# Kernel study: the diagonal 32x32 blocks of the GDN inverse solved on GpSimd beside the local attention

## The chip, the core and the metric

The kernel runs on one core of a Trainium2 chip. The metric is device time in microseconds (us), the median of several runs; here 2867.46 us over three runs (2866.38 to 2867.61). The profile is one execution with its own span.

## The reference, cut to what matters

Two transformer blocks in float32 on 512 positions. The change is in the even layer of the second, which has a gated delta rule (GDN, 6 heads of width 128) beside a dilated local attention. The delta rule solves, for each head and chunk of positions, a unit lower triangular system:

```
decay = jnp.exp(jnp.where(incl, gam[..., :, None] - gam[..., None, :], -jnp.inf))
kk = jnp.einsum('bhnid,bhnjd->bhnij', kc, kc)
lower = jnp.eye(c) + jnp.where(strict, bc[..., :, None] * kk * decay, 0.0)
sol = lax.linalg.triangular_solve(lower, rhs, left_side=True, lower=True, unit_diagonal=True)
...
delta = u_n - jnp.einsum('bhck,bhkv->bhcv', w_n, state)
o_n = jnp.einsum('bhck,bhkv->bhcv', qd_n, state) + jnp.einsum('bhij,bhjv->bhiv', qk_n, delta)
state = gl_n[..., None, None] * state + jnp.einsum('bhck,bhcv->bhkv', kd_n, delta)
```

## The kernel before

The program is a row of regions, each with a barrier of all five engines behind it: a region ends when its last engine ends, and SyncE has to have issued its DMAs. Inside a region each engine has its own list of instructions, in order, with semaphores between them. Three regions and the start of a fourth matter here.

**The residual region** ends with the projections of the even layer. Weights come in pieces of 128x1024: SyncE loads them into one of three `raw` buffers (`W.load`, L205), ScalarE rounds them to a high part (`split_high`, L220), VectorE or GpSimd forms the rest (`split_low`, L230), into four buffers each. A load into a used `raw` waits for the low part three pieces earlier. At this region's end the first four pieces of the next projection (`even_out`) are already split and three more are loaded.

**The window region** (`window_region`) is the local attention: 8 units, each with scores (L1476, L1480) on TensorE, logits on VectorE, exponentials on ScalarE, 12 transposes (`turn`, L1491) and 24 products with the values (L1509). SyncE brings bias tables, level masks and the small table `pick`. GpSimd has no work here.

**The recurrence region** (`recurrence_region`) walks four chunks (n = 0 to 3) of 128 positions, with the six heads in two groups g of three. For a chunk it needs the inverse of the 128x128 triangular matrix I - M. `MT` holds M transposed, `TT` the transposed inverse, `T` the inverse. Level 0 sets 2x2 blocks (`first_level`, L2613 and L2616); each of the levels 1 to 6 doubles the size of the finished diagonal blocks:

- GpSimd masks `MT` into `BT` (`masked`, L2721);
- TensorE multiplies `T` with `BT` (`a`, L2366), ScalarE copies the result to `W1` (`product`, L2497);
- TensorE multiplies `W1` with `TT` (`b`, L2374), VectorE adds that to `TT` (`sums`, L2642);
- TensorE transposes `TT` (`turn_inverse`, L2380) and ScalarE copies it to `T` (`inverse`, L2502); not on level 6.

In the spaces of the levels (`beside`) TensorE runs the state steps of the chunk before (s1 to s4 and `head_sums`, L2317 to L2356) and the preparation of the chunk after (p1 to p7, L2248 to L2303), all in PSUM banks 6 and 7. The preparation needs copies by ScalarE (`decays`, `betas`, `key_rows` L2470, `value_rows` L2481, `inverse_start` L2490), sums by VectorE (`decays`, `kept`, `matrix`, `scores`, `queries`, `keys`) and products by GpSimd (`factors` L2731, `decayed_betas` L2737). Chunk 0 is prepared ahead of the loop, the prologue. Behind chunk 3 there is a tail: one long logarithm on ScalarE (L2564), then `delta`, `output`, `square` and the last logarithms (L2572).

**The layer region** starts with `even_out`, whose first products (L292) need split weights.

A three-head product of two 128x128 matrices shows as six matmul records in the trace, since each float32 matmul is two; a three-head transpose shows as three. In the order listings below, which count instructions as written, both are x3.

## Time and profile before

| | us |
|---|---|
| median of three runs | 2867.46 |
| profiled execution, first to last instruction | 2866.3 |
| TensorE busy | 2653.8 (93%) |
| VectorE busy | 1494.4 (52%) |
| ScalarE busy | 1085.4 (38%) |
| GpSimd busy | 438.2 (15%) |
| window region | 62.0 (1485.1 to 1547.1) |
| recurrence region | 174.8 (1547.1 to 1721.9) |

Times inside the span are counted from its first instruction. The two regions are 8% of the span. Busy shares of the whole program say little about them: what counts there is how full TensorE is in each stretch, and which engine a region's last instruction waits for.

### The profile page before, as it was taken

To read this page: it belongs to the slowest core of one execution; us is meant where nothing else is said; L and a number is where in the kernel's file an instruction comes from. 1 tells how busy PE (TensorE), PEld (TensorE's weight loads), DVE (VectorE), ACT (ScalarE), POOL (GpSimd) and SP (SyncE) were. 2 spreads that over 40 slices of the span, in tenths; PEclk is the share of its full clock that TensorE was granted. 3 is DMA by queue.
4 is the path that set the end of the run, shared out by engine and by line. 5 is a ranking of instruction groups with operands and counts; after the bars stand their busy time and mean duration, and the time that the engine had idled before them with its cause. 6 is when DMAs were issued, how large, how long until landed. Compare 5 with 4: busy or idle time off the path is not lost. (4 is left out here: it accounts for less than half of the span.)

```text
span 2866.3 us, 32688 instructions
## 1 busy us (share of the span) xinstructions
PE 2653.8 (93%) x12838; PEld 2117.6 (74%) x12838; DVE 1494.4 (52%) x2141; ACT 1085.4 (38%) x1659; POOL 438.2 (15%) x356
## 2 busy tenths in 40 slices
PE   8998998799999999969988998999998988899997
PEld 5676887577778888746777886887776865687775
DVE  5644553454456653365434545677634345676743
ACT  5653443533432322334323454322224446422223
POOL 4544442000000000000001433000020031200002
PEclk9998899999999999989998999999999999999999
DMA  6233002333023323222220001222332310122231
GB/s 216 92 107 118 1 1 84 112 103 103 23 88 103 96 90 94 74 74 74 81 88 1 1 1 52 81 88 91 108 95 93 96 45 30 57 90 89 88 109 61
DMA packets 82624, 222.06 MB, mean 77 GB/s; under 512 B 13293, under 2 KB 29949, under 8 KB 81283
## 3 DMA queue, kind: packets, MB, share of 16 engines
q1 hardware_dynamic: 78112, 205.49, 22.4%
q10 hardware_dynamic: 4360, 14.49, 1.4%
q8 instruction: 103, 1.69, 0.2%
q14 instruction: 49, 0.40, 0.0%
HBM read 213.60 MB, written 11.58 MB: 79 GB/s over the span
## 5 line engine op out<-in xcount | busy, mean ns | idle before, releaser
L230 DVE TENSOR_TENSOR w_low<-w_raw,w_high 128x1024 fp32r<-128x1024 f32 (+2 forms) x341 | 410.8, 1206 | 874.2 <-ACT w_high L220 874.0
L292 PE MATMUL bank<-x_high,w_high 128*128 128x512 f32 x1840 | 742.7, 404 | 32.2 <-DVE x_low L486 20.4
L293 PE MATMUL bank<-x_low,w_high 128*128 128x512 f32 x1840 | 734.5, 399 | 0.0
L294 PE MATMUL bank<-x_high,w_low 128*128 128x512 f32 x1840 | 731.2, 397 | 0.0
L220 ACT ACTIVATE w_high<-w_raw 128x1024 fp32r<-128x1024 f32 (+2 forms) x380 | 386.3, 1019 | 620.5 <-PE bank L294 502.4
L292 PEld LDWEIGHTS bank<-x_high,w_high 128*128 128x128 f32 x1840 | 349.0, 190 | 142.4 <-issue 53.0
L293 PEld LDWEIGHTS bank<-x_low,w_high 128*128 128x128 f32 x1840 | 349.0, 190 | 87.8 <-issue 5.5
L294 PEld LDWEIGHTS bank<-x_high,w_low 128*128 128x128 f32 x1840 | 348.6, 189 | 83.1
L294 PE MATMUL bank<-f_high,w_low 128*128 128x512 f32 x528 | 209.9, 397 | 0.0
L292 PE MATMUL bank<-f_high,w_high 128*128 128x512 f32 x528 | 208.8, 395 | 0.9 <-DVE w_low L230 0.9
L293 PE MATMUL bank<-f_low,w_high 128*128 128x512 f32 x528 | 208.4, 395 | 0.0
L292 PEld LDWEIGHTS bank<-f_high,w_high 128*128 128x128 f32 x528 | 99.1, 188 | 27.1 <-issue 3.0
L293 PEld LDWEIGHTS bank<-f_low,w_high 128*128 128x128 f32 x528 | 99.1, 188 | 25.3 <-issue 0.5
L294 PEld LDWEIGHTS bank<-f_high,w_low 128*128 128x128 f32 x528 | 99.1, 188 | 23.2
L230 POOL TENSOR_TENSOR w_low<-w_raw,w_high 128x1024 fp32r<-128x1024 f32 x39 | 95.3, 2443 | 127.4 <-ACT w_high L220 127.3
L403 POOL TENSOR_TENSOR ln_half<-x 128x512 f32<-128x512 f32 x4 | 6.9, 1718 | 690.9 <-DVE x L3672 690.9
L3585 ACT ACTIVATE f_high<-gate 128x512 fp32r<-128x512 f32 x44 | 27.8, 632 | 215.0 <-DVE gate L3703 215.0
L292 PE MATMUL bank<-o_high,w_high 128*128 128x512 f32 x192 | 79.4, 414 | 10.3 <-DVE o_low L555 10.3
L3582 ACT ACTIVATE gate<-gate 128x512 f32<-128x512 f32 x44 | 27.8, 632 | 155.1 <-DVE gate L717 155.1
L293 PE MATMUL bank<-o_low,w_high 128*128 128x512 f32 x192 | 78.1, 407 | 0.0
L294 PE MATMUL bank<-o_high,w_low 128*128 128x512 f32 x192 | 77.9, 406 | 0.0
L1022 DVE TENSOR_TENSOR raw<-bank,rstd 128x512 f32<-128x512 f32 x38 | 25.9, 687 | 95.2 <-PE bank L294 75.8
(605 smaller groups left out, 4090.2 us busy)
## 6 DMA issues: line engine op xcount, KB each, us to landing
w_raw<-in_ffn_in_dram SPq DMA_DIRECT2D x132, 512.0 KB, 3.3
w_raw<-in_ffn_out_dram SPq DMA_DIRECT2D x48, 512.0 KB, 3.5
w_raw<-in_gdn_in_dram SPq DMA_DIRECT2D x24, 512.0 KB, 3.3
w_raw<-in_mix_in_dram SPq DMA_DIRECT2D x22, 512.0 KB, 4.3
w_raw<-in_ffn_out_dram SPq DMA_DIRECT2D x24, 384.0 KB, 3.1
w_raw<-in_swa_qk_dram SPq DMA_DIRECT2D x12, 512.0 KB, 3.3
bias_rows<-bias_row ACTq DMA_DIRECT2D x4, 1280.0 KB, 13.8
w_raw<-in_mix_gate_a_dram SPq DMA_DIRECT2D x8, 512.0 KB, 3.3
```

The costliest lines, as they stand in the source:

```text
L220: self.nc.scalar.activation(self.high[c % SPLIT][:, 0:w], self.raw[c % RAW][:, 0:w], ACT.Copy).then_inc(self.high_done, 1)
L230: (on or self.nc.vector).tensor_tensor(self.low[c % SPLIT][:, 0:w], self.raw[c % RAW][:, 0:w], self.high[c % SPLIT][:, 0:w].bitcast(F32), ...
L292: nc.tensor.matmul(out, wh, high[:, k, :], start=first + at == 0, stop=False)
L293: nc.tensor.matmul(out, wh, low[:, k, :], start=False, stop=False)
L294: last = nc.tensor.matmul(out, wl, high[:, k, :], start=False, stop=first + at == depth - 1)
L403: self.nc.gpsimd.tensor_tensor(self.half[:], self.x[:, 0, :], self.x[:, 1, :], ALU.add).then_inc(self.S["half_ok"], 1)
L1022: W.freed(nc.vector.tensor_tensor(raw[i % 3][:], W.bank(PS, name, n)[:], rstd[:], ALU.mult), name, n)
L3582: nc.scalar.activation(g[i % 2][:], g[i % 2][:], ACT.Silu).then_inc(R["act_ready"], 1)
L3585: nc.scalar.activation(FH[:, i, :], g[i % 2][:], ACT.Copy).then_inc(R["f_high"], 1)
```

## The change

1. **Window region.** TensorE also computes K K^T for the four 32x32 diagonal blocks of every head and chunk (`key_edges`: 96 matmuls of 32x32 outputs) between the first and the second scores. ScalarE copies them out. SyncE writes `gam` and `beta` to HBM and reads them back by block (2 and 8 DMAs), writes the blocks to HBM in runs of 128 bytes (4 DMAs) and reads them back as 96 partitions of 1024 numbers, one block in each. GpSimd forms decays and signs, and solves the 96 unit triangular blocks by forward substitution (`solve_edges`: 30 steps of a product and a sum). The result goes to HBM and comes back as `TC` (1 and 4 DMAs, the last four waited for in the next region). The scratch for it is the memory of the high and low weights.
2. **Residual and recurrence region, weights.** The four pieces of `even_out` are therefore split in the recurrence region: ScalarE in slots 3 to 6 of the last chunk, GpSimd at its own end.
3. **Recurrence region.** Two doubling levels are left (32 to 64, 64 to 128). Each chunk has seven slots; slot s holds p(s+1) of the chunk after, and the state steps of the chunk before stand in slots 0 to 3 and 5. The p steps use banks 1 and 4. `first_level` is one product that spreads the solved blocks. GpSimd makes both masks of a group together, in the order factors, masked, decayed_betas.

The diff below is cut to its core; each `@` names the function and the engine, and long arguments are shortened.

```diff
@solve_edges
+    for j in range(1, EDGE - 1):
+        w = EDGE - 1 - j
+        part = TMP[rows, 0:j * w].rearrange("p (s t) -> p s t", t=w)
+        pool.wait_ge(step, j)
+        nc.gpsimd.tensor_tensor(part, X[:, 0:j, j:j + 1].broadcast_to(both), X[:, j:j + 1, j + 1:].broadcast_to(both),
+                                ALU.mult).then_inc(product, 1)
+        pool.wait_ge(product, j)
+        nc.gpsimd.tensor_tensor(X[:, 0:j, j + 1:], X[:, 0:j, j + 1:], part, ALU.add).then_inc(step, 1)
@window_region, sync
+            sp.wait_ge(R["keys_copied"], 2)
+            for b in range(B):
+                sp.dma_start(inner["keys_flat"][b].rearrange("m s t -> s m t"), ...).then_inc(R["keys_out"], 16)
+            sp.wait_ge(R["keys_out"], 16 * B)
+            sp.dma_start(KB[rows, :], inner["keys_flat"].rearrange("b m s t -> (b m) (s t)")).then_inc(R["keys_in"], 16)
+            sp.wait_ge(R["solved"], 1)
+            sp.dma_start(inner["solved_flat"].rearrange("b m s t -> (b m) (s t)"), SOL[rows, :]).then_inc(...)
+            sp.wait_ge(R["solved_out"], 16)
+            for b in range(B):
+                sp.dma_start(TC[...], inner["solved_flat"][b].rearrange("m s t -> s m t")).then_inc(inner["solved_in"], 16)
@window_region, scalar
+                if u == 1:
+                    act.wait_ge(R["gap"], 2)
+                    nc.scalar.activation(DEC[rows, :], DEC[rows, :], ACT.Exp).then_inc(R["edge_decay"], 1)
@recurrence_region, tensor
+                for slot in range(7):
+                    for g in range(G):
+                        if slot == 0: a(n, 0, g)
+                        if slot == 1: b(n, 0, g)
+                        if slot == 2: turn_inverse(n, g)
+                        if slot == 3: a(n, 1, g)
+                        if slot == 4: b(n, 1, g)
+                        if before >= 0: ...   # s1, s2, s3, s4, -, head_sums in slots 0 to 5
+                        if after < NT:
+                            (p1, p2, p3, p4, p5, p6, p7)[slot](after, g)
@recurrence_region, scalar
+                    if after == NT and slot >= 3:
+                        W.split_high(act, W.end("swa_v") + slot - 2)
@recurrence_region, vector
-                nc.vector.tensor_tensor(TT, MT, mask[:, 0:1, :], ALU.mult)
-                nc.vector.tensor_tensor(TT, TT, C["ident"], ALU.add)
+                nc.vector.tensor_tensor(TT, edges[:, a:b, n, None, :].broadcast_to(shape), mask[:, 0:1, :], ALU.mult)
@recurrence_region, gpsimd
+                for g in range(G):
+                    factors(n, g)
+                for g in range(G):
+                    masked(n, g)
+                    decayed_betas(n, g)
+            pool.wait_ge(R["tt0"], at(NT - 1, G - 1))
+            W.split_low(pool, W.end("swa_v") + SPLIT, nc.gpsimd)
@residual_region
-            W.load(sp, W.end("swa_v") + SPLIT + RAW)
+            W.load(sp, W.end("swa_v") + RAW)
-                W.split_high(act, W.ahead("swa_v", gr))
+                W.split_high(act, min(W.ahead("swa_v", gr), W.end("swa_v")))
```

TensorE at the start of the window region before (scores of units 0 and 1, the turn of unit 0):

```order
L1476 MATMUL bank<-swa_qk_6800 128x512 x2
L1480 MATMUL bank<-swa_qk_6800 128x128 x4
L1476 MATMUL bank<-swa_qk_6800 128x512 x2
L1480 MATMUL bank<-swa_qk_6800 128x128 x4
L1491 MATMUL bank<-ident,window_logits_12173 128x128 x12
```

and after, where the 96 products of `key_edges` (L1578) stand between the scores of the first two units:

```order
L1529 MATMUL bank<-swa_qk_6808 128x512 x2
L1533 MATMUL bank<-swa_qk_6808 128x128 x4
L1578 MATMUL bank<-qkvz_6810 32x32 x96
L1529 MATMUL bank<-swa_qk_6808 128x512 x2
L1533 MATMUL bank<-swa_qk_6808 128x128 x4
L1546 MATMUL bank<-ident,window_logits_12160 128x128 x12
```

The turn of unit 0 (L1491 before, L1546 after) is now behind 96 more matmuls.

TensorE in chunk 1 before, level 1 and the start of level 2 (L2366 is `a`, L2374 is `b`, L2380 `turn_inverse`, L2317 s1, L2248 p1 and L2250, L2251 its small parts, L2326 s2):

```order
L2366 MATMUL bank<-t_12756,bt_12757 128x128 x3
L2317 MATMUL bank<-state_12765,qkvz_6802 128x128 x3
L2366 MATMUL bank<-t_12756,bt_12757 128x128 x3
L2317 MATMUL bank<-state_12765,qkvz_6802 128x128 x3
L2374 MATMUL bank<-tt_12752,w_243_12758 128x128 x3
L2248 MATMUL bank<-gam_6804,pick_12172 128x128 x3
L2250 MATMUL bank<-ident,gam_6804 128x6
L2251 MATMUL bank<-ident,beta_6803 128x6
L2374 MATMUL bank<-tt_12752,w_243_12758 128x128 x3
L2380 MATMUL bank<-ident,tt_12752 128x128 x3
L2248 MATMUL bank<-gam_6804,pick_12172 128x128 x3
L2380 MATMUL bank<-ident,tt_12752 128x128 x3
```

and after, slots 0 and 1 (L2449 is `a`, L2457 `b`, L2403 s1, L2349 p1, L2410 s2, L2359 p2):

```order
L2449 MATMUL bank<-t_13017,bt_13018 128x128 x3
L2403 MATMUL bank<-state_13026,qkvz_6810 128x128 x3
L2349 MATMUL bank<-gam_6812,pick_12152 128x128 x3
L2351 MATMUL bank<-ident,gam_6812 128x6
L2352 MATMUL bank<-ident,beta_6811 128x6
L2449 MATMUL bank<-t_13017,bt_13018 128x128 x3
L2403 MATMUL bank<-state_13026,qkvz_6810 128x128 x3
L2349 MATMUL bank<-gam_6812,pick_12152 128x128 x3
L2457 MATMUL bank<-tt_13014,w_251_13019 128x128 x3
L2410 MATMUL bank<-rhs_13023,tt_13013 128x128 x3
L2359 MATMUL bank<-beta_6811,pick_12152 128x128 x3
L2457 MATMUL bank<-tt_13014,w_251_13019 128x128 x3
```

`a` and `b` are now in different slots, with three more steps of both groups between them, and no transpose stands in the first two slots.

ScalarE at the end of chunk 3 before (L2497 `product`, L2524 `sums_read`, L2564 the long logarithm, L2509 `delta`):

```order
L2497 ACTIVATE w_243_12758<-bank 128x384
L2524 ACTIVATE qkvz_6802<-bank 128x3x128
L2497 ACTIVATE w_243_12758<-bank 128x384
L2524 ACTIVATE qkvz_6802<-bank 128x3x128
L2502 ACTIVATE t_12756<-bank 128x384 x2
L2497 ACTIVATE w_243_12758<-bank 128x384 x2
L2564 ACT_TABLE_LOAD
L2564 ACTIVATE qkvz_6802<-qkvz_6802,rms_eps 128x6x384
L2509 ACTIVATE delta_12763<-bank 128x384 x2
```

and after (L2564 is now `product`, L225 the high part of a weight piece, L2592 `sums_read`, L2635 the long logarithm, L2577 `delta`):

```order
L2564 ACTIVATE w_251_13019<-bank 128x384
L2588 ACTIVATE rhs_13023<-o_even_12150 128x384
L225 ACTIVATE w_high_5_49<-w_raw_1 128x1024
L225 ACTIVATE w_high_6_50<-w_raw_2 128x1024
L2592 ACTIVATE qkvz_6810<-bank 128x3x128 x2
L225 ACTIVATE w_high_7_51<-w_raw_3 128x1024
L225 ACTIVATE w_high_8_52<-w_raw_1 128x1024
L2635 ACT_TABLE_LOAD
L2635 ACTIVATE qkvz_6810<-qkvz_6810,rms_eps 128x6x384
L2577 ACTIVATE delta_13024<-bank 128x384 x2
```

Four pieces of weights now stand ahead of the long logarithm, and the fourth uses `w_raw_1` a second time.

## Rows read from the trace of the kernel before

**Rows 1.** Stretches: window region, prologue, chunks 0, 1 and 3.

```profile
core 0: us, PE busy (x) PEld busy (x) DVE busy (x) ACT busy (x) POOL busy (x), PEclk, DMA share, GB/s
1485.06:1547.10 62.04, 54.99 (x392) 48.48 (x392) 25.40 (x88) 26.96 (x51) 0.01 (x1) 0.91 0.08 21
1547.10:1567.50 20.40, 17.12 (x70) 14.53 (x70) 10.79 (x23) 6.91 (x23) 7.39 (x7) 0.50 0.00 0
1567.50:1603.20 35.70, 32.15 (x246) 29.28 (x244) 18.50 (x34) 16.79 (x46) 16.85 (x16) 0.96 0.00 1
1603.20:1639.90 36.70, 35.26 (x288) 32.84 (x287) 20.64 (x43) 18.19 (x46) 14.41 (x14) 1.00 0.01 2
...
1676.60:1713.80 37.20, 35.98 (x290) 32.72 (x288) 17.50 (x31) 21.45 (x50) 15.07 (x14) 1.00 0.00 1
```

**Rows 2.** The longest wait in total in the four chunks, 1567 to 1714.

```profile
POOL bt L2721 <- PE bank L2366: 73.0, 35, 4.7
```

**Rows 3.** TensorE weight loads in order of time (start, us, what), chunk 1.

```profile
1612.25 0.75 PEld L2366 LDWEIGHTS bank<-t,bt 128*128 128x128 f32 x6
1612.92 0.75 PEld L2326 LDWEIGHTS bank<-rhs,tt 128*128 128x128 f32 x6
...
1624.23 0.36 PEld L2380 LDWEIGHTS bank<-ident,tt 128*128 128x128 f32 x3
1624.57 0.75 PEld L2344 LDWEIGHTS bank<-delta,k_rows 128*128 128x128 f32 x6
```

**Rows 4.** ScalarE in order of time, end of the residual region.

```profile
1480.49 1.06 ACT L220 ACTIVATE w_high<-w_raw 128x1024 fp32r<-128x1024 f32 x1 [4.58 <-PE bank L317]
```

**Rows 5.** TensorE on 32-column products in order of time, and that stretch's clock.

```profile
2327.53 1.93 PE L2916 MATMUL bank<-k_about,q_blocks 128*32 128x128 f32 x32
...
2327.00:2330.00 3.00, 2.47 (x36) 1.38 (x32) 0.47 (x1) 0.63 (x4) 1.45 (x4) 0.50 0.02 5
```

**Rows 6.** TensorE in order of time, first turn of the window.

```profile
1492.42 2.74 PE L1491 MATMUL bank<-ident,window_logits 128*128 128x128 f32 x12
```

**Rows 7.** DMA: issues by SyncE, packets from 20 to 30 us, landing of 512 KB.

```profile
1485.06 3.65 SPq L1464 DMA_DIRECT2D g_bias<-bias_rows  x8
...
q1 hardware_dynamic: 3026, 1.23, 45.7%
...
w_raw<-in_gdn_in_dram SPq DMA_DIRECT2D x24, 512.0 KB, 3.3
```

**Rows 8.** GpSimd groups by shape: busy, mean ns, idle before.

```profile
L230 POOL TENSOR_TENSOR w_low<-w_raw,w_high 128x1024 fp32r<-128x1024 f32 x39 | 95.3, 2443 | 127.4 <-ACT w_high L220 127.3
...
L2845 POOL TENSOR_TENSOR k_about<-k_far,far_decay 128x224 f32<-128x224 f32 x4 | 2.6, 656 | 0.0
...
L2845 POOL TENSOR_TENSOR k_about<-k_far,far_decay 128x64 f32<-128x64 f32 x4 | 1.2, 296 | 0.0
```

**Rows 9.** GpSimd in order of time, 2367 to 2370.

```profile
2367.25 0.72 POOL L2832 TENSOR_TENSOR k_about<-k_near,gla_qkr 128x256 f32<-128x256 f32 x1
2368.12 1.53 POOL L2838 TENSOR_TENSOR q_blocks<-q_about,gla_qkr 64x256 f32<-64x256 f32 x2
```

**Rows 10.** One instruction each of ScalarE, GpSimd, VectorE in chunk 1.

```profile
1621.19 0.49 ACT L2497 ACTIVATE w<-bank 128x384 f32<-128x384 f32 x1 [0.18 <-PE bank L2366]
...
1621.24 1.00 POOL L2721 TENSOR_TENSOR bt<-mt,level_mask 128x384 f32<-128x384 f32 x1 [1.57 <-PE bank L2366]
...
1623.21 0.56 DVE L2642 TENSOR_TENSOR tt<-tt,bank 128x384 f32<-128x384 f32 x1 [2.40 <-PE bank L2374]
```

**Rows 11.** ScalarE in order of time: value rows of chunk 1, end of chunk 3, tail.

```profile
1601.80 0.97 ACT L2481 ACTIVATE v_rows<-bank,col 128x128 f32<-128x128 f32 x3
...
1712.25 1.28 ACT L2564 ACT_TABLE_LOAD   x1
...
1715.67 0.85 ACT L2509 ACTIVATE delta<-bank 128x384 f32<-128x384 f32 x2
...
1721.29 0.58 ACT L2572 ACTIVATE qkvz<-bank,rms_eps 128x384 f32<-128x384 f32 x1 [0.59 <-PE bank L2356]
```

More of the change, by code:

```diff
@@ L1458, in window_region @@
     with region(nc, "bias0", "bias1", "scores", "near", "logits", "exp", "turned", "copied", "copied_last", "inv", "values", "rows", "final",
-                "o") as (block, R):
+                "o", "keys", "keys_copied", "flat", "edge_gates", "keys_out", "keys_in", "covered", "gap", "edge_decay", "signed",
+                "product", "step", "solved", "solved_out") as (block, R):
         @block.sync
@@ L1516, in finish, with key_edges @@
                 last.then_inc(R["final"], 1)
+            def key_edges():
+                for m in range(M):
+                    h, n = m // NT, m % NT
+                    for b in range(B):
+                        k = K[:, h, n * P + EDGE * b:n * P + EDGE * b + EDGE]
+                        last = nc.tensor.matmul(
+                            PS[4 + m // 16][EDGE * b:EDGE * b + EDGE, EDGE * (m % 16):EDGE * (m % 16) + EDGE], k, k,
+                            start=True, stop=True)
+                    if m in (15, M - 1):
+                        last.then_inc(R["keys"], 1)
             for u in range(N + 2):
@@ L2666, in gated @@
                                                of(3, n, g), ALU.mult, ALU.mult).then_inc(R["og"], 1)
-            for prepare in (decays, kept, matrix, first_level, scores, queries, keys):
+            for prepare in (decays, kept, matrix, scores, queries, keys, first_level):
                 for g in range(G):
@@ L2672, in _ @@
                 before, after = n - 1, n + 1
[L2673 to L2689 removed]
+                for slot in range(7):
@@ L2703, in _ @@
-                        if before >= 0 and level == 5 and after < NT:
+                            if slot == 5:
+                                keys(after, g)
+                        if slot == 4:
+                            sums(n, 1, g)
+                        if after < NT and slot == 4:
+                            queries(after, g)
+                            first_level(after, g)
+                        if before >= 0 and slot == 5:
                             gated(before, g)
+                        if after == NT and slot == 6:
+                            rhs(n, g)
```

443 lines of the change are left out of this document (228 added, 215 removed).

## Prediction

> **What bounds the kernel now.** I read the table by stretches first. In chunks 1 and 3 of the recurrence TensorE is busy 35.3 of 36.7 us and 36.0 of 37.2 us at full clock [rows 1]; in the other engines' columns of the same rows nothing exceeds 22 us. So the loop is bound by TensorE's own list of work, and the waits say the same from the other side: GpSimd's masks wait for TensorE, 73 us in total [rows 2]. The pitch of that list is in the weight loads: a three-head product starts 0.67 us after the one before it, a three-head transpose is followed after 0.34 us [rows 3]. Whatever work is taken from TensorE there comes off the time, until a chain of waits is longer. The window region is different: 62.0 us, GpSimd empty, VectorE and ScalarE under half [rows 1]. It is free for GpSimd, but its barrier waits for SyncE and GpSimd too, and the change gives both a long chain.
>
> **The change, part by part.** The sum is made in the profiled execution (2866.3 us); the median of the runs is 1.2 us above it.
>
> *Residual region.* The high part of a weight piece at 1480.49 stands ahead of the last copies [rows 4]; it goes, and they start when TensorE ends at 1480.4. -1.0 us, below 0 and not under -2: nothing is added there.
>
> *Window region.* I count T from its start (before: next region at T = 62.0). TensorE's new 96 products are 192 records. The nearest row is a 32-column product, 32 records in 1.93 us at half clock, (1.93 - 0.27) / 31 = 0.054 us each [rows 5]. That gives 10.3 us (bounds 5 at full clock, 21 if the column groups don't overlap: 0.11 us each), from T = 3.0 to 13.3, copied at 14.1. The first turn then starts near T = 15.5, not 7.4 [rows 6]: the attention ends 8.1 us later, less some 1.5 us for a turn and scores that ran at half clock before and may be at full clock by then, and the next region could start at T = 68.7.
>
> The chain of the blocks: four DMAs of 768 runs, issued at 3.65 / 8 = 0.46 us each from T = 14.2. Small packets took 0.457 x 160 us / 3026 = 24 ns of one engine [rows 7], so 3072 take 4.6 us over 16 engines; with 2.0 us to land, T = 20.8 (bounds 0 and +7 for packets up to 60 ns). The read back lands 3.3 us after its issue [rows 7]: T = 24.5. Decays and signs (8 DMAs behind `flat`, three passes over 1024 numbers, one exponential) I put ready at T = 23, so not last. First product, 128x1024: 2.44 us [rows 8], T = 27.0. Then 60 instructions over 9920 numbers in all. From 64 to 224 numbers costs (656 - 296) / 160 = 2.25 ns each, fixed part 0.15 us [rows 8]: 60 x 0.15 + 9920 x 0.00225 = 31.3 us. Each waits for the one before it; the gap in such a place is 2368.12 - 2367.97 = 0.15 us, and 0.07 inside the pair behind it [rows 9]: 0.1 x 60 = 6.0. T = 64.3. Diagonal, write back (3.3), four issues (1.8), barrier (0.9): T = 70.8. The chain is last, by 2 us over the attention. Window region +8.8 us, bounds +4 (solve at 28, key products at full clock) and +23 (gaps 0.15, slow packets, 0.1 us more per instruction).
>
> The Trainium skill ("DMA: Bandwidth & Descriptors", Specifications) says that transfers under 512 bytes are done as read-modify-write. The small packets of [rows 7] are loads into SBUF; no row here shows small stores to HBM, of which the change makes 3072. If stores took twice as long, the sum would be 4.6 us higher. It speaks against the change but does not turn it; it is a rival below.
>
> *Recurrence, prologue.* 20.4 us before [rows 1]. GpSimd now makes four masks ahead of the second `decayed_betas` (2 x 1.0 us more), `keys` and then `first_level` follow it. I follow the chain: second mask pair done 2.3 us later than the old `decayed_betas`, first_level cheaper. +2.4 us (0 to +5). The landing of `TC` (issued before the barrier, some 7 us) is hidden by the 20 us of this prologue; if it weren't, it would cost what it is late.
>
> *Chunks.* Removed per chunk: 4 levels x 2 groups x (a and b) = 16 products x 0.67 = 10.7 us, 8 transposes x 0.34 = 2.7 us. TensorE's list for a full chunk is 36.7 - 13.4 = 23.3 us including the stalls of before, about 22.0 by counting: 26 products, 8 transposes, 2 head sums and small parts. Then I walked the seven slots with each engine's durations (ScalarE 0.49, GpSimd 1.0, VectorE 0.56 [rows 10], and up to 1.0 for what reads two SBUF tiles). Slots 0 to 4 run without a stall: `b` of a group comes 3 us after its `a`, and the copy between takes 0.7. In slots 5 and 6 TensorE has only 2.6 us of work, while ScalarE must do key rows, sums and value rows of both groups, 0.97 us for each set of rows [rows 11]: transpose, rows, transpose, `t`. There the second group's last transpose waits for `v_rows`. +1.6 us: 23.8 us per full chunk, for chunks 1 and 2: 2 x -12.9 = -25.8 us (each between 22.2, TensorE's list alone, and 30, where every slot takes the 4.3 us of the fullest).
>
> Chunk 0 has no state steps, so its TensorE list is only 14 us and the chain of preparation steps sets the time: 18.4 us by the same walk. It starts at half clock as before (0.50 in the prologue, [rows 1]), for which I add 3.6: 22.0 for 35.7, -13.7 us (18.5 to 29).
>
> Chunk 3 and tail were 1676.6 to 1721.9 = 45.3 us. Now: five slots of `a`, `b`, state steps end near 13 us, but ScalarE has four weight pieces ahead of the long logarithm. The fourth uses a `raw` that SyncE may fill only when GpSimd has done the first low part: high at 13.2, low 2.44 us [rows 8] at 15.7, load 3.3 us [rows 7] at 19.0, high 1.06 [rows 4] at 20.1. Then the table load and the logarithm, 1715.67 - 1712.25 = 3.4 us, and `delta` starts at 23.6; from there to the end 1721.9 - 1715.7 = 6.2 us as before [rows 11]. 29.8 us: -15.5 (bounds -19, if the load is early enough, and -12). Half of what the removed levels could give is lost here to a new wait for a load.
>
> Sum: -1.0 + 8.8 + 2.4 - 13.7 - 25.8 - 15.5 = -44.8; 2866.3 - 44.8 = 2821.5, and 1.2 more for the median: 2822.7 us, 1.6% faster. I say 2823. Its own range is 2812 to 2835.
>
> **Rivals.**
> - *The attention hides the chain and the chunks run at TensorE's list.* Window +4, chunks 1 and 2 at 22.2, chunk 3 -19, chunk 0 -17: about 2808. For it: the chain is last by 2 us only. Against it: the two-engine chains in slots 5 and 6.
> - *GpSimd is dearer on narrow rows than on rows of 16 numbers.* L2845 has inner rows of 16; the solve goes down to 1. With 0.3 us more on each of 60 instructions the chain ends at T = 89, net -27: 2841.
> - *Small stores are slow*: +4.6 us by the price above, 2827.
> - *The recurrence becomes bound by latency, or TensorE falls to half clock in it.* The clock was 0.50 in all of the prologue, where TensorE stalled [rows 1]. Full chunks of 30 us, chunk 0 of 29, chunk 3 two more, near the upper bound of each part: +21, 2844. Against it: the walk finds one stall of 1.6 us.
> - *Slower than before.* The place is the barrier of the window region: each microsecond by which GpSimd's solve is longer goes straight to the end. The gain elsewhere is 53.6 us, so the region would have to end at T = 115.6, the solve at 82 us, 1.37 us for each instruction. The nearest rows are 0.30 and 0.66 us [rows 8]. At 1.5 us each: solve 90 us, 2876. Only a new kind of cost could do it.
>
> **Chances.** Forecast 0.55; attention hides it 0.12; narrow rows 0.11; small stores 0.06; latency or clock 0.12; slower 0.03; something else, near no change, 0.01. The range 2807 to 2845 leaves out the last two and the ends of the others. 0.2% (6 us) is about what a measurement can tell from no change. Faster 0.96, same 0.01, slower 0.03.
>
> **What would show it.** The next region starts 70 to 72 us after the window region's start, GpSimd's last add is the last wait there, and its adds and products take 0.2 to 0.7 us. The 192 small records take about 10 us and the first turn starts near T = 15.5. Full chunks take 23 to 25 us with TensorE above 90% until `key_rows`. ScalarE waits for `w_raw` ahead of the fourth high part. The forecast is wrong if GpSimd's gaps or durations are twice these, if TensorE's clock is 0.5 in a chunk, or if VectorE waits for `TC` at the end of the prologue.

## The result, and the profile after

The changed kernel takes 2821.23 us (median of 4 runs, 2820.41 to 2827.58), the kernel before 2867.49 in the same session: ratio 0.9837, 95% interval 0.9821 to 0.9852, 1.6% faster. The profiled execution is 2820.41 us with a span of 2818.6. Forecast were 2823 and 2807 to 2845.

The table of stretches of the changed kernel: window region, prologue, chunks 0, 1 and 2, and all from chunk 3 to the start of the next region. They answer to [rows 1]; columns as there.

```profile
1481.78:1547.80 66.02, 59.08 (x584) 51.81 (x584) 25.30 (x88) 28.66 (x54) 42.02 (x72) 0.89 0.18 41
1547.80:1569.77 21.97, 16.70 (x70) 14.34 (x70) 9.04 (x21) 6.91 (x23) 9.30 (x9) 0.58 0.00 1
1569.77:1595.23 25.46, 24.18 (x125) 21.68 (x125) 10.97 (x24) 10.02 (x30) 7.35 (x7) 0.65 0.00 1
1595.23:1619.64 24.41, 23.62 (x191) 21.58 (x189) 15.20 (x34) 13.51 (x38) 9.42 (x10) 1.00 0.00 1
1619.64:1644.14 24.50, 23.71 (x190) 21.67 (x189) 16.40 (x36) 13.50 (x38) 8.99 (x9) 1.00 0.01 1
...
1644.14:1676.14 32.00, 23.36 (x173) 20.82 (x171) 15.34 (x24) 19.70 (x32) 11.13 (x5) 0.95 0.20 66
```

The last stretch ends here with the first product of the next region, in the kernel before at 1724.60:

```profile
1676.60:1724.60 48.00, 42.14 (x329) 37.46 (x328) 20.18 (x35) 28.84 (x61) 15.07 (x14) 0.99 0.00 1
```

The forecast took it to the last logarithm (1721.9) on both sides, which leaves the change comparable.

Against the kernel before (us):

| stretch | before | after | change | forecast |
|---|---|---|---|---|
| up to the window region | 1485.06 | 1481.78 | -3.3 | -1.0 |
| window region | 62.0 | 66.0 | +4.0 | +8.8 |
| prologue | 20.4 | 22.0 | +1.6 | +2.4 |
| chunk 0 | 35.7 | 25.5 | -10.2 | -13.7 |
| chunks 1 and 2 | 73.4 | 48.9 | -24.5 | -25.8 |
| chunk 3 to the next region | 48.0 | 32.0 | -16.0 | -15.5 |
| the rest | 1141.7 | 1142.5 | +0.8 | 0 |

The first row is no clean result: eleven experiments run the same program up to there, and their window regions start between 1483.09 and 1490.74. Nor is the size of the second: in seven profiles that leave this region alone, the changed kernel's among them, it takes 63.8 to 66.2 us, and in a second profile of the old region 61.0. The full chunks are what was forecast: TensorE 23.6 of 24.4 us busy at full clock. The places that deserve a look are the window region, whose +4.0 hides two errors, and chunk 0, where the granted clock is 0.65. That clock is no accident of one execution: the eight profiled kernels with the changed kernel's orders in prologue and chunk 0 take 25.1 to 25.8 us for chunk 0.

GpSimd in the window region of the changed kernel, in order of time: the decays, the first product, the first step and the last sum. Only GpSimd's rows are shown; a bracket holds the idle time ahead of a row and what ended it.

```profile
1495.86 2.77 POOL L1697 TENSOR_SCALAR edge_decay<-edge_decay 96x1024 f32<-96x1024 f32 x1
1499.87 2.37 POOL L1700 TENSOR_TENSOR edge_decay<-edge_decay,edge_gates 96x1024 f32<-96x1024 f32 x1 [1.24 <-ACT edge_decay L1625]
1502.38 2.35 POOL L1704 TENSOR_TENSOR edge_inverse<-edge_blocks,edge_decay 96x1024 f32<-96x1024 f32 x1
1504.81 0.23 POOL L1456 TENSOR_TENSOR edge_part<-edge_inverse 96x30 f32<-96x30 f32 x1
1505.12 0.23 POOL L1459 TENSOR_TENSOR edge_inverse<-edge_inverse,edge_part 96x30 f32<-96x30 f32 x1
...
1539.09 0.26 POOL L1459 TENSOR_TENSOR edge_inverse<-edge_inverse,edge_part 96x30 f32<-96x30 f32 x1
...
1547.80 0.74 POOL L2781 MEMSET state<- 128x768 f32 x1 [8.23 <-POOLq L551]
```

The substitution takes 34.5 us, from 1504.81 to 1539.35, not 37.3: the gap between two dependent instructions is 0.08 us, the cheapest takes 0.23. The last product and sum, 30 rows of one number, take 0.25 and 0.26 us, the first, one row of 30, 0.23 each: narrow rows cost next to nothing. But GpSimd then waits 8.23 us at the barrier. SyncE, behind it, is done at T = 62.8 (T from the region's start); the region ends at T = 66.0. So the solve isn't last in this execution. TensorE and ScalarE in the same region show what is:

```profile
1484.75 1.93 PE L1578 MATMUL bank<-qkvz 128*32 128x32 f32 x192
...
1489.36 1.53 PE L1546 MATMUL bank<-ident,window_logits 128*128 128x128 f32 x12 [0.16 <-ACT edge_keys L1621]
...
1500.79 4.22 PE L1564 MATMUL bank<-swa_v,window_turned 128*128 128x64 f32 x24 [0.95 <-issue]
1504.80 2.77 PE L1546 MATMUL bank<-ident,window_logits 128*128 128x128 f32 x12
...
1545.05 0.66 PE L1570 MATMUL bank<-ident,window_rows 128*128 128x128 f32 x4 [0.45 <-DVE window_rows L1660]
```

```profile
1498.66 1.06 ACT L1625 ACTIVATE edge_decay<-edge_decay 96x1024 f32<-96x1024 f32 x1 [5.70 <-POOL edge_decay L1697]
1499.63 1.06 ACT L1601 ACTIVATE window_turned<-bank 128x512 f32<-128x512 f32 x2
...
1545.74 1.07 ACT L1629 ACTIVATE o_even<-bank 128x512 f32<-128x512 f32 x1 [4.63 <-PE bank L1570]
```

The 192 key records take 1.93 us, 0.010 us each, at a granted clock of 0.94; in the kernel with the products done twice, below, they ran at 0.50 and took 2.79 us. The first turn starts at T = 7.6 (before: 7.4). What holds the attention is ScalarE's 5.70 us of waiting for GpSimd's decays, in front of the copies of unit 1 (1499.63). TensorE, which turned that unit at 1496.25 to 1497.73, stands idle behind them and then does the next transposes in 2.77 us instead of 1.48, at half clock.

The prologue and the start of chunk 0, TensorE in order of time, and the granted clock (seventh value, ahead of the DMA share) in pieces of 4 us:

```profile
1564.02 0.55 PE L2385 MATMUL bank<-ident,qkvz 128*128 128x128 f32 x3 [0.21 <-ACT k_rows L2537]
1568.32 1.51 PE L2392 MATMUL bank<-ident,tt 128*128 128x128 f32 x6 [3.76 <-DVE tt L2687]
1569.77 1.65 PE L2449 MATMUL bank<-t,bt 128*128 128x128 f32 x6
```

```profile
1560.00:1564.00 4.00, 3.73 (x16) 2.69 (x15) 2.08 (x5) 1.81 (x7) 2.07 (x3) 0.57 0.00 0
1564.00:1568.00 4.00, 0.55 (x3) 0.31 (x3) 2.10 (x3) 1.51 (x6) 3.05 (x3) 0.86 0.00 0
1568.00:1572.00 4.00, 3.68 (x15) 3.14 (x16) 0.64 (x2) 1.47 (x3) 0.00 (x0) 0.50 0.00 0
...
1584.00:1588.00 4.00, 4.00 (x23) 4.00 (x23) 1.58 (x3) 1.52 (x5) 2.00 (x3) 0.58 0.00 0
```

TensorE waits 3.76 us for the solved blocks in TT, which VectorE copies only behind the keys, and these wait for GpSimd's second decayed betas. The clock rises to full shortly ahead of this wait, falls back within it (near 1567), and stays at half until 1587: 17 of the 25.5 us of chunk 0, in which TensorE is busy all the time.

The tail, ScalarE from the fourth high part on, and VectorE's products ahead of rhs:

```profile
1662.71 1.06 ACT L225 ACTIVATE w_high<-w_raw 128x1024 fp32r<-128x1024 f32 x1 [2.83 <-DMA w_raw<-in_even_out_dram]
1663.79 1.28 ACT L2635 ACT_TABLE_LOAD   x1
1665.08 2.22 ACT L2635 ACTIVATE qkvz<-qkvz,rms_eps 128x2304 f32<-128x2304 f32 x1
1667.20 0.85 ACT L2577 ACTIVATE delta<-bank 128x384 f32<-128x384 f32 x2
```

```profile
1657.63 4.90 DVE L2739 SCALAR_TENSOR_TENSOR o_even<-o_even,gdn_norm,qkvz 128x384 f32<-128x384 f32 x2
1662.45 1.00 DVE L2725 TENSOR_TENSOR rhs<-v_rows,bank 128x384 f32<-128x384 f32 x2
...
1670.45 0.62 DVE L2739 SCALAR_TENSOR_TENSOR o_even<-o_even,gdn_norm,qkvz 128x384 f32<-128x384 f32 x1 [6.99 <-ACT rhs L2588]
```

The wait for the fourth weight piece is there, and `delta` starts 23.1 us into chunk 3 (23.6 forecast). The first row of VectorE is two products in 4.90 us; the same product takes 0.62 at 1670. GpSimd's four low parts (1657.13 to 1667.05) run beside the slow ones. `rhs`, which has one of its two inputs in PSUM, runs beside them too and takes 0.50 us each.

### The profile page after: what moved, and what is told of

Read it like the earlier page. It is cut to its first block and busy times, and to the rows that moved or that the text cites. A ratio compares the mean times of both kernels' runs of the same rounds, so it can differ in the third digit from the quotient of the medians.

```text
span 2818.6 us, 31986 instructions
## 1 busy us (share of the span) xinstructions
PE 2605.4 (92%) x12550; PEld 2070.7 (73%) x12550; DVE 1464.8 (52%) x2097; ACT 1057.6 (38%) x1598; POOL 457.9 (16%) x399
## 5 line engine op out<-in xcount | busy, mean ns | idle before, releaser
L297 PE MATMUL bank<-x_high,w_high 128*128 128x512 f32 x1840 | 746.9, 406 | 32.1 <-DVE x_low L491 20.4
L225 ACT ACTIVATE w_high<-w_raw 128x1024 fp32r<-128x1024 f32 (+2 forms) x380 | 386.2, 1019 | 603.1 <-PE bank L299 502.0
L235 POOL TENSOR_TENSOR w_low<-w_raw,w_high 128x1024 fp32r<-128x1024 f32 x43 | 105.2, 2448 | 141.1 <-ACT w_high L225 141.0
L297 PE MATMUL bank<-o_high,w_high 128*128 128x512 f32 x192 | 78.4, 408 | 10.3 <-DVE o_low L560 10.3
L1027 DVE TENSOR_TENSOR raw<-bank,rstd 128x512 f32<-128x512 f32 x38 | 25.8, 686 | 96.6 <-PE bank L299 77.2
```

What stands on the lines that cost most here:

```text
L225: self.nc.scalar.activation(self.high[c % SPLIT][:, 0:w], self.raw[c % RAW][:, 0:w], ACT.Copy).then_inc(self.high_done, 1)
L235: (on or self.nc.vector).tensor_tensor(self.low[c % SPLIT][:, 0:w], self.raw[c % RAW][:, 0:w], self.high[c % SPLIT][:, 0:w].bitcast(F32), ...
L297: nc.tensor.matmul(out, wh, high[:, k, :], start=first + at == 0, stop=False)
L1027: W.freed(nc.vector.tensor_tensor(raw[i % 3][:], W.bank(PS, name, n)[:], rstd[:], ALU.mult), name, n)
```

## The experiments

Times are set against the 2821.23 us of the changed kernel; sizes of a few us are read from the stretches of the profiles, since runs of one kernel spread by up to 7 us.

### Is the solve last in the window region?

**Solve shortened** (28 of its 30 steps left out):

```diff
-    for j in range(1, EDGE - 1):
+    for j in (1, 2):
```

> The changed kernel with 2 of the 30 steps of the substitution (4 of 60 GpSimd instructions); the other steps are left out, so the blocks are not inverses. GpSimd's chain ends 30 us earlier. Theory A (the attention, held by the wait for the decays, ends last): the region stays at 66.0 us (within 0.5), and the total near 2821. Theory S (the solve's chain ends last): the region shrinks by what the chain stood over the attention, 2 us by the prediction, more if the attention had not been delayed.

Measured: the region keeps 66.16 us, while GpSimd now waits 41.48 us at the barrier. 2823.09 us. Its attention was last, and theory S, my prediction's own, is out for it: the last transposes start at T = 63.4, as in the changed kernel. Two executions further down with the changed kernel's own orders in this region had the solve last.

```profile
1484.29:1550.45 66.16, 59.06 (x584) 52.03 (x585) 25.31 (x88) 28.66 (x54) 13.19 (x16) 0.89 0.18 41
```

**Every product twice:**

```diff
+        for i in range(2):
-        nc.gpsimd.tensor_tensor(part, X[:, 0:j, j:j + 1].broadcast_to(both), X[:, j:j + 1, j + 1:].broadcast_to(both),
-                                ALU.mult).then_inc(product, 1)
-        pool.wait_ge(product, j)
+            nc.gpsimd.tensor_tensor(part, X[:, 0:j, j:j + 1].broadcast_to(both), X[:, j:j + 1, j + 1:].broadcast_to(both),
+                                    ALU.mult).then_inc(product, 1)
+            pool.wait_ge(product, 2 * j - 1 + i)
```

> The changed kernel with every product of the substitution done twice, each waiting for the one before it: 90 GpSimd instructions for 60. The second product gives the same numbers. The 60 took 34.5 us with gaps of 0.08 us, so the 30 more should add about 17 us to the solve. Theory A: the chain of the solve (last issue at T = 62.8) stood 2 to 3 us ahead of the attention's end, so the region grows by 17 - 3 = about 14 to 15 us, to 80 to 81, and GpSimd or SyncE is the last wait. If the solve's chain was already last (theory S), the region grows by the whole 17 us. If wider gaps or a wait of another kind bound each instruction, the added time per product differs from 0.57 us.

Measured: 2840.86 us. SyncE's issue behind the solve comes at T = 74.7 (1563.65 - 1488.93) instead of 57.8: 16.9 us for 30 products, 0.56 each with its gap. The region grows by 14.7 us, so 2.2 us of the solve had been hidden in the changed kernel's profile; beyond that each microsecond goes to the end, as the rival "slower" had it. ScalarE waits for the decays here too, 5.18 us, but TensorE stays at full clock behind the wait, and its last transposes start at T = 58.6 (1547.50 - 1488.93) instead of 63.3.

```profile
1547.50 0.66 PE L1571 MATMUL bank<-ident,window_rows 128*128 128x128 f32 x4 [0.45 <-DVE window_rows L1661]
...
1488.93:1569.69 80.76, 55.24 (x585) 48.62 (x585) 25.31 (x88) 28.43 (x54) 56.51 (x102) 0.84 0.14 33
```

**The exponential of the decays behind the copies of unit 1** (ScalarE):

```diff
                 if 1 <= u <= N:
                     copies(u - 1)
+                if u == 2:
+                    act.wait_ge(R["gap"], 2)
+                    nc.scalar.activation(DEC[rows, :], DEC[rows, :], ACT.Exp).then_inc(R["edge_decay"], 1)
                 if u < N:
                     exponentials(u)
...
-                if u == 1:
-                    act.wait_ge(R["gap"], 2)
-                    nc.scalar.activation(DEC[rows, :], DEC[rows, :], ACT.Exp).then_inc(R["edge_decay"], 1)
```

> The changed kernel with ScalarE's exponential of the block decays moved from behind the exponentials of unit 1 to behind the copies of unit 1 in the window region. ScalarE waited 5.70 us for GpSimd there, and the turned tiles of unit 1, ready at about 1497.3, were copied at 1499.63. Theory A (the attention ended last): the copies start 2.3 us earlier, the exponential still starts at 1498.7, the solve isn't later, and the region shrinks from 66.0 to 64 us (TensorE's last transposes at T = 61.3 instead of 63.3); the solve's last DMA issue at T = 62.8 becomes the near tie. Theory S (my prediction: the solve's chain ends last): the region stays at 66.0, because the chain's end is the same.

Measured: TensorE's last transposes start at T = 57.2 (1542.31 - 1485.13) instead of 63.3. That is 6.1 us, three times the 2.0 expected, because half clock went with the wait: some 3 us right behind it, and 1.6 more in a later stretch (1523 to 1530 in the changed kernel) that the kernel before also had at half clock (1526.20). The region shrinks by 1.3 us only, to 64.73, because now the solve is last: SyncE's last issue ends at T = 63.7, the next region begins 1.0 later. Median 2820.98 (ratio 0.9837, 0.9822 to 0.9851): by itself not to be told from the changed kernel.

```profile
1542.31 0.66 PE L1570 MATMUL bank<-ident,window_rows 128*128 128x128 f32 x4 [0.46 <-DVE window_rows L1660]
...
1485.13:1549.86 64.73, 54.31 (x584) 48.35 (x585) 25.30 (x88) 28.59 (x54) 41.97 (x72) 0.93 0.18 41
```

The comparison of two profiles makes the order look better than it is. Nine kernels of this study keep the changed kernel's order on ScalarE and its 192 records. Their last transposes start at T = 58.6 to 63.4; the half clock behind the wait is there in all but the one with products twice. The wait by itself costs 1.4 us at most (58.6 against 57.2), the rest is the clock. In the kernels with the blocks ahead of the keys and with the wide products first (both below) they start at 60.1 and 60.2, the solve is last, as GpSimd's short wait at the barrier shows, and the region takes 63.8 us, less than with the decays moved:

```profile
1544.49 0.66 PE L1570 MATMUL bank<-ident,window_rows 128*128 128x128 f32 x4 [0.46 <-DVE window_rows L1660]
...
1548.10 0.74 POOL L2781 MEMSET state<- 128x768 f32 x1 [6.02 <-POOLq L551]
...
1484.35:1548.14 63.79, 55.97 (x584) 49.99 (x585) 25.31 (x88) 28.55 (x54) 41.97 (x72) 0.93 0.18 42
```

So in the seven profiles that leave the region alone attention and solve end within 2.5 us of each other, and the later one changes with the clock behind the wait. With the exponential moved the region takes 64.7 us here and 64.2 in the last kernel below, within the 63.8 to 66.2 of the old order: no run shows a gain for the region.

### What does a key product cost?

**Each key product four times:**

```diff
-                        last = nc.tensor.matmul(
+                        for _ in range(4):
+                            last = nc.tensor.matmul(
```

> The changed kernel with each of TensorE's 96 key products done four times: 768 records for 192, all else as it is. The 192 took 1.93 us at full clock. If the price is 0.010 us for one record, the 576 more take 5.8 us and the first turn moves from T = 7.6 to 13.4. The prediction's price, 0.054, would give 31 us more. Theory A: ScalarE's wait for the decays (5.7 us at unit 1) hides 2.3 us or more of it, so the region grows by 2 to 4 us, not 5.8.

Measured: 2841.22 us; the region is 80.07 us. The records of TensorE:

```profile
1490.76 4.70 PE L1579 MATMUL bank<-qkvz 128*32 128x32 f32 x207
1496.73 2.71 PE L1579 MATMUL bank<-qkvz 128*32 128x32 f32 x128 [1.27 <-issue]
1500.20 2.71 PE L1579 MATMUL bank<-qkvz 128*32 128x32 f32 x128 [0.76 <-issue]
```

They take 22.4 us (1490.76 to 1513.16), not 7.7: my expectation was wrong. In the changed kernel the group of 32 columns changes with every product, that is after two records; here 8 records in a row go to the same group, and the pitch is 2.71 / 128 = 0.021 us instead of 0.010, at full clock. The eight also have the same operands and the same output, and no run separates that from the group. And this long list waits for its issue after each 128 records, 0.8 to 1.3 us. The last transposes start 14.0 us later (T = 77.3, 1565.35 - 1488.06), the records take 20.5 us more: ScalarE no longer waits for the decays, as theory A had it, and the half clock behind that wait is gone too.

### What holds chunk 0?

**The stall filled in part** with transposes that nobody reads:

```diff
+            for i in range(13):
+                nc.tensor.transpose(PS[6][:, chunk(i % 3)], C["ident"][:], C["ident"][:])
             for g in range(G):
                 p7(0, g)
```

> The changed kernel with 13 transposes of the identity into an unused bank on TensorE, between the last value transposes of the prologue and the first transpose of TT, where TensorE stood idle for 3.76 us (1564.57 to 1568.32). Nothing else moves; they take about 13 x 0.275 = 3.6 us at half clock. Theory H (half clock): the stall is what kept TensorE at 1.2 GHz until 1587, and chunk 0 (25.5 us) was bound by TensorE at that clock. With the stall filled the clock rises within about 5 us of chunk 0's start, as in the kernel before, and chunk 0 takes 18 to 21 us: 5 to 7 us less, about 2815. Rival K (chain): the chain of preparation steps sets chunk 0, as I predicted, and the clock adds little: chunk 0 stays within 1 us of 25.5 even if the clock rises. Rival N: the clock doesn't depend on this stall: it stays at 0.5 to about 1587, and nothing changes.

**The copies of the solved blocks ahead of the keys** (VectorE, prologue):

```diff
-            for prepare in (decays, kept, matrix, scores, queries, keys, first_level):
+            for prepare in (decays, kept, matrix, scores, queries, first_level, keys):
```

> The changed kernel with one order changed on VectorE: in the prologue of the recurrence the copies of the solved blocks into TT (first_level) stand ahead of the scaling of the keys, which waits for GpSimd's second decayed betas. Direct effect: first_level can run at 1563.0 to 1564.1 instead of 1567.6, TensorE's transposes of TT start near 1564.8 instead of 1568.3 and chunk 0 starts near 1566.3: 3.4 us earlier. Theory H: with the stall gone the clock rises early as well, so chunk 0 is 5 to 7 us shorter too: 8 to 10 us in all, about 2812. Rival N (the clock doesn't follow from the stall): -3.4 only, or, if the rise at 1587 stays where it is, about -1.7, since half of the work moved forward runs at half clock. Rival K (the chain sets chunk 0): -3.4 and chunk 0 still 25 us.

Measured: 2819.89 us (ratio 0.9830, 0.9815 to 0.9845) and 2814.03 us (0.9816, 0.9798 to 0.9834). Prologue and chunk 0 of the first, then of the second:

```profile
1549.33:1570.92 21.59, 17.72 (x83) 15.24 (x83) 9.04 (x21) 7.02 (x24) 9.27 (x9) 0.64 0.00 1
1570.92:1593.05 22.13, 20.85 (x125) 18.68 (x126) 10.98 (x24) 9.94 (x30) 7.36 (x7) 0.77 0.00 1
```

```profile
1548.14:1566.36 18.22, 16.03 (x70) 13.73 (x71) 9.32 (x20) 6.79 (x23) 8.28 (x8) 0.58 0.02 4
1566.36:1588.38 22.02, 20.74 (x126) 18.56 (x125) 12.21 (x26) 10.00 (x30) 8.96 (x9) 0.77 0.00 1
```

In the first kernel the stall was only shortened: the clock had risen ahead of it, so the 13 transposes took 1.58 us (1565.90), not 3.6, and TensorE still waited 2.34 us:

```profile
1569.82 0.99 PE L2392 MATMUL bank<-ident,tt 128*128 128x128 f32 x6 [2.34 <-DVE tt L2691]
```

Chunk 0 is 3.3 and 3.4 us shorter at a clock of 0.77, and the second kernel gains 3.7 in the prologue. Half of theory H: the clock does set chunk 0, but it didn't stay up. In both it rose ahead of the chunk (near 1565 and 1564) and fell again for about 10 us within it. The median of the first isn't to be told from the changed kernel's; the second's is 7.2 us lower, with intervals that just overlap.

**The kernel before, with a stall:**

```diff
+            for t in (R_, U, W1):
+                nc.vector.tensor_tensor(t[:], MT[0][:], MT[0][:], ALU.mult).then_inc(R["late"], 1)
...
+            pe.wait_ge(R["late"], 3)
             for g in range(G):
                 p7(0, g)
```

> The kernel before, with a stall put into the prologue of its recurrence: VectorE does three more products of 768 numbers into tiles that are free there, and TensorE waits for them ahead of the first transposes of TT (at 1566.06 before). They should end near 1569.8, so chunk 0 starts 3.5 to 4 us later. Theory H (TensorE's stall at this place costs the full clock for the first part of chunk 0): the clock, which before rose at about 1570, rises 15 to 20 us later, and chunk 0 takes 6 to 9 us more than its 35.7, so 10 to 13 us in all. Rival N (something else of the change holds the clock, such as GpSimd's or the DMA queues' work): chunk 0 keeps its 35.7 us and only the 4 us of the stall show.

Measured: 2871.13 us. TensorE waits 3.14 us; prologue 23.56 us (+3.2, of which 0.2 is where the stretch was cut), chunk 0 35.96 (+0.3), clock 0.96 as before [rows 1]. Theory H fails in this kernel: a stall at this place is not enough. Here, as in the kernel before, the clock was 0.50 through the whole prologue and rose once, some 4 us after the stall. In the changed kernel it had risen ahead of the stall and fell in it.

```profile
1546.38:1569.94 23.56, 17.16 (x70) 14.67 (x70) 13.40 (x26) 6.91 (x23) 7.41 (x7) 0.50 0.00 1
...
1569.94:1605.90 35.96, 32.41 (x245) 29.56 (x245) 18.49 (x34) 16.79 (x46) 16.86 (x16) 0.96 0.00 1
```

**Wide products first** (the changed kernel, TensorE's order in slot 0 of chunk 0):

```diff
+            for g in range(G):
+                a(0, 0, g)
...
-                        if slot == 0:
+                        if slot == 0 and n:
                             a(n, 0, g)
```

> The changed kernel with both first products a of chunk 0 (128 rows each) ahead of the two spreads of chunk 1 (products with 6 rows), on TensorE alone; the stall of 3.76 us ahead of the first transposes of TT stays. After that stall TensorE then does 4.7 us of 128-row work at half clock without a break, about what the kernel before with a stall put in did (4.2 us) when its clock rose at 26 us after the region's start; in the changed kernel it rose at 39.5. Theory G (the narrow products of chunk 0's first slots, which the seven slots put between the wide ones, keep the clock low): the clock rises at 25 to 28 us and chunk 0 takes 19 to 21 us instead of 25.5. Rival P (what comes first in the chunk doesn't matter, only where the stall lies): the clock stays at half to about 39, and chunk 0 stays at 25 to 26.

Measured: chunk 0 22.26 us at a clock of 0.76; but a median of 2821.87 us (0.9838, 0.9820 to 0.9856), no gain. The clock rises near 1574.7, 25.6 us after the region's start, as theory G had it; but it falls again near 1578 and stays at half to about 1585, which no theory had. What a chunk gains in one profiled execution doesn't show in the median. Inconclusive.

### What holds the tail?

**The logarithm ahead of the third and fourth high part** (ScalarE); in the second kernel also **rhs ahead of the last gated products** (VectorE); in the third the latter alone:

```diff
-                    if after == NT and slot >= 3:
+                    if after == NT and slot in (3, 4):
                         W.split_high(act, W.end("swa_v") + slot - 2)
...
...
             # behind the long logarithm
+            W.split_high(act, W.end("swa_v") + 3)
             for g in range(G):
                 delta(n, g)
+            W.split_high(act, W.end("swa_v") + 4)
```

```diff
-                        if before >= 0 and slot == 5:
+                        if after < NT and before >= 0 and slot == 5:
                             gated(before, g)
                         if after == NT and slot == 6:
                             rhs(n, g)
+                    if after == NT and slot == 6:
+                        for g in range(G):
+                            gated(before, g)
```

> The changed kernel with ScalarE's order at the end of the recurrence changed: two high parts, head sums, then the long logarithm, the third high part, delta of the last chunk, the fourth high part. ScalarE waited 2.83 us for the load of the fourth piece ahead of the table load, and delta started at 1667.20. Theory W (the wait for w_raw, as predicted, sets the tail): delta can start when TensorE has done s2, at 1665.2 to 1666 instead of 1667.2, so the next region starts 1 to 2 us earlier. It can't be the 3 us of the wait, since s2 itself starts only at 1663.05 behind VectorE's rhs. Rival V (VectorE's gated products ahead of rhs set the tail): no change over 0.5 us.

> As the kernel with the logarithm moved ahead of the third and fourth high part, and VectorE's rhs of the last chunk ahead of the two gated products of chunk 2, which took 4.90 us beside GpSimd's low parts (2.45 us each; 0.62 without them) and held rhs until 1662.45. Both ends of the tail are then free: rhs near 1660.4, s2 of TensorE to 1662.5, the logarithm done at 1662.4, the third high part at 1663.5, delta from there: 3.7 us earlier than 1667.2, and the next region starts 3.5 us earlier, if two waits of equal length (V and W) held the tail together. Each alone gives 0 to 1.5. If another wait is behind both (the last low part of GpSimd, which now comes later, or the barrier), less.

> The changed kernel with VectorE's rhs of the last chunk ahead of the two gated products alone; the logarithm stays behind the fourth high part. TensorE's s2 can start 2.5 us earlier, but delta waits for ScalarE, which waits for the load of the fourth weight piece and then does the logarithm (to 1667.2, 23.0 us after the start of chunk 3). If both waits hold the tail in parallel, delta stays where it is and the last stretch keeps 32.0 us (up to 34.4, as other executions of the same orders had). If VectorE's order alone set it, 2.5 us less.

Measured, from chunk 3 to the next region: 30.19, 28.11 and 34.51 us; medians 2822.19 (0.9836, 0.9820 to 0.9853), 2818.01 (0.9821, 0.9805 to 0.9838), and 2830.04 in a single run, whose window region starts 9.0 us later than the changed kernel's, ahead of any change. No median here is clear of the changed kernel's. The changed orders of other experiments leave this stretch alone, and there it takes 32.0 to 34.4 us. The spread lies behind the start of `delta`: from there to the next region it is 8.9 us where the clock stays full and 9.6 to 11.4 in the other executions, at a granted clock of 0.75 to 0.86. The start of `delta` is the cleaner reading. It is 23.1 us into chunk 3 with rhs alone (1676.44 - 1653.37), as without it, where all kernels with the old orders lie at 23.1 to 23.4; 20.6 with the logarithm alone (1667.16 - 1646.57), where ScalarE waits for TensorE's s2 and this for VectorE's rhs; and 19.2 with both (1665.92 - 1646.75). So ScalarE's queue is the last wait, and VectorE's order the one right behind it.

```profile
1653.37:1687.88 34.51, 24.39 (x173) 22.02 (x171) 14.99 (x24) 19.68 (x32) 11.13 (x5) 0.90 0.17 61
```

```profile
1646.75:1674.86 28.11, 22.01 (x172) 19.59 (x171) 14.20 (x24) 19.57 (x32) 10.56 (x5) 1.00 0.23 75
```

### Together

The four new orders in one kernel: decays later, blocks ahead of keys, logarithm first, rhs first.

> The changed kernel with the four new orders together: the exponential of the block decays behind the copies of unit 1, first_level ahead of the keys in the prologue, the logarithm ahead of the third and fourth high part, and rhs ahead of the last gated products. Each has been run on its own or in a pair: the window region went from 66.0 to 64.7 us, prologue and chunk 0 from 47.4 to 40.2, the tail from 32.0 (up to 34.4 in other executions) to 28.1. If they add up: 1.3 + 7.2 + 3.9 = 12.4 us under the changed kernel, about 2809. If the clock gives one of them back in the next stretch (an execution with a tail 2 us longer had the rest of the program 2.3 us shorter), 2811 to 2813. Over 2815 the parts don't add up.

Measured: 2808.01 us (5 runs, 2806.56 to 2812.53), ratio 0.9794, interval 0.9780 to 0.9808, clear of the changed kernel's. It beats both kernels. The total is the expected one, the parts are not: against the changed kernel the window region gives 1.8 us (64.18), prologue and chunk 0 10.2, the tail 2.3 (29.73), where 1.3, 7.2 and 3.9 were expected. `delta` starts 19.2 us into chunk 3 as before; the tail's rest is the spread named above. End of the prologue and chunk 0:

```profile
1547.27:1561.00 13.73, 12.54 (x54) 11.73 (x55) 4.83 (x15) 3.10 (x10) 4.83 (x5) 0.50 0.03 5
1561.00:1565.48 4.48, 3.07 (x18) 1.77 (x17) 4.48 (x6) 3.58 (x13) 3.43 (x3) 0.96 0.00 0
1565.48:1584.47 18.99, 16.63 (x126) 14.47 (x125) 12.04 (x26) 9.89 (x30) 8.97 (x9) 1.00 0.00 1
```

Here the clock rises near 1562 and stays, and chunk 0 takes 18.99 us: close to the 18.4 that the walk gave for a chain of preparation steps at full clock. The prologue and chunk 0 have the same orders as in the kernel with the blocks ahead of the keys, where the clock fell again and the chunk took 22.02. So the orders in these two stretches don't set the clock's course alone. The two kernels also differ ahead of them, in the window region, and each has one profile: whether that region decides it or chance stays open. The Trainium skill ("TensorE: Matmul & The Clock Gate", What's actually happening) says that the number of matmuls ahead of the clock's first rise differs from run to run of one kernel. With the changed kernel's own orders the clock's course through the prologue and chunk 0 hardly varied: 25.1 to 25.8 us in eight profiles.

## Why the prediction was right, and where it wasn't

- *Sum.* -44.8 against -47.7 in the spans. Of the 2.9 us between them 2.3 lie ahead of the window region, where equal programs differed by up to 9 us. The main mechanism holds: the removed levels came off chunks bound by TensorE's list. That the total lies within 2 us of the forecast is partly luck: the window region came out 4.8 us under its term, chunk 0 3.5 us over its own.
- *Residual region.* The copies do start when TensorE ends; the size can't be told from the spread.
- *Window region, key products.* The term was mis-sized: 10.3 us, measured 1.93. [rows 5] has products that move 128 columns at half clock, 0.054 us a record; here 32 columns move, 0.010 us a record near full clock and 0.015 at half (2.79 / 192). I carried the time over without the columns. So three signs failed: the records took 2 us, not 10, the first turn started at T = 7.6, not 15.5, and the next region at T = 66.0, not 70 to 72.
- *Window region, decays.* The step "I put them ready at T = 23, so not last" was wrong twice. GpSimd was done with them at T = 20.5 (1502.24), but the keys' way back into SBUF had been issued at T = 14.4 (24.5 forecast for its end) and no longer counted. And I looked only at who needs the decays, not at who stands behind ScalarE's wait for them: the attention. That wait and the half clock around it are 6.1 us in the changed kernel's profile (1.4 for the wait alone), which roughly replaced the 8.1 us that the key products were to cost.
- *Window region, solve.* Right in size: 34.5 us for 37.3. Wrong in time: with the keys early its last issue ended at T = 62.8, some 7 us earlier than the forecast had it. The claim that it is last held in two of seven profiles of this region and failed in the changed kernel's own, where it ended 2.2 us under the attention. With the forecast for the region at +8.8 and +4.0 measured, the rival "attention hides the chain" (+4) gave this term, though for another reason.
- *Small stores and narrow rows.* Neither showed. The read back was issued 1.6 us behind the last store's issue (1494.52 to 1496.14).
- *Prologue and chunk 0.* +1.6 for +2.4 in the prologue, by the chain that was named (second mask pair, decayed betas, keys, blocks). In chunk 0 the term for the clock was mis-sized: I took "half clock as before" and put it at 3.6 us. Before, the clock rose 2.5 us into the chunk; here it rose 17 us into it. At full clock the chunk takes 18.99, in the changed kernel 25.46, so it was 6.5. My sign "TensorE's clock is 0.5 in a chunk" came true for two thirds of this one, and only here. Why the clock stayed low is open.
- *Chunks 1 and 2.* 24.4 and 24.5 us for 23.8. TensorE's list is 23.6, not 22.0, and the waits for `v_rows` 0.8 instead of 1.6: two errors that nearly cancel.
- *Chunk 3 and tail.* Right: the wait for `w_raw` is there, 2.83 us, and taking it out of `delta`'s way starts `delta` 2.5 us earlier. Not seen: VectorE's slow products as the wait behind it.

## What to carry to other kernels

When an engine gets a new wait, list what is queued behind it on that engine as carefully as who provides what it waits for: ScalarE's wait, with the half clock that mostly came behind it, cost the attention 1.4 to 6.2 us, all 192 new products 1.93. A chain placed beside other work is free only to its slack, here 2.2 us of 62.8 in one execution and nothing in another, and two waits that end together have to be moved together. Before a change of 1 or 2 us in a stretch is called a gain, look at the same stretch in other profiles of the same orders. A price taken from another line must be scaled by the columns that move and by the clock at which it was read.

## What the runs showed of the hardware

- Products with 32 moving columns cost 0.010 us a record when products go to the four groups of 32 columns in turn, 0.021 when four equal products in a row stay in one group. The Trainium skill ("TensorE: Matmul & The Clock Gate", Wait — 56ns, not 53.3ns?) gives about 25 ns as the least distance between two matmuls however few columns they have; that is near the value in one group, and over twice the value over four.
- A GpSimd product or sum costs 0.23 us at 30 numbers of a partition and 0.61 to 0.69 at 240, down to rows of one number; the gap between dependent ones is 0.08 us. With one input and 1024 numbers it is not cheaper: 2.77 us against 2.35.
- VectorE's products of 384 numbers with two SBUF inputs took 2.45 us each beside GpSimd's low parts and 0.62 without them; `rhs`, with one SBUF and one PSUM input, took 0.50 beside them. The Trainium skill ("GPSIMD Engine Reference", 8. Key points) names contention between the two engines for instructions with two SBUF inputs; this row has the price.
- TensorE's clock was full through most of an idle stretch in the prologue and then at half for 17 us in which the engine was busy all the time. What decides this is open: it isn't the stall alone, nor what stands first in the chunk.
